# VectorE's order at the last tile of a MoE layer: the third group of experts chosen ahead of the last norms, the last router product a block later, list scatters paused at each tile

## The chip, the cores and the metric

The kernel runs on one core of one Trainium2 chip. The metric is the device time of one execution in microseconds (us), the median of the runs shown.

## What is computed

One layer of a hybrid backbone on T = 1152 tokens (1024 sample tokens and 128 prompt tokens) of width D = 1024: adaLN, a mixer (gated linear attention, a gated MLP, a short convolution, a Fourier branch), a residual with layer norm, then a mixture of 64 experts with a shared expert and a second residual with layer norm. The change lies where the mixer's output meets the mixture:

```python
x = layer_norm(DEEPNORM_ALPHA * x + g1 * y, p["ln1_g"], p["ln1_b"])
h = layer_norm(x) * (1 + sc2) + sh2
...
scores = jax.nn.sigmoid((x @ p["w_router"]).astype(jnp.float32))
biased = scores + p["router_bias"].astype(jnp.float32)
grp_score = lax.top_k(biased.reshape(t, N_GROUPS, EXPERTS_PER_GROUP), 2)[0].sum(-1)
_, top_g = lax.top_k(grp_score, TOPK_GROUPS)
gmask = jnp.any(top_g[:, :, None] == jnp.arange(N_GROUPS)[None, None, :], axis=1)
masked = jnp.where(jnp.repeat(gmask, EXPERTS_PER_GROUP, axis=1), biased, -jnp.inf)
_, idx = lax.top_k(masked, TOP_K)
w = jnp.take_along_axis(scores, idx, axis=1)
...
return (jax.nn.silu(xb @ p["w_exp_gate"][e]) * (xb @ p["w_exp_up"][e])) @ p["w_exp_down"][e]
...
shared = (jax.nn.silu(x @ p["w_sh_gate"]) * (x @ p["w_sh_up"])) @ p["w_sh_down"]
return (routed + shared).reshape(bsz, n, d)
```

Each token goes to 8 of 64 experts, which come from 4 of 8 groups. The assignments are sorted by expert and cut into blocks of 128 rows, each padded to one expert.

## The kernel before, in words

**Tiles and blocks.** Tokens are cut into NT = 9 tiles of 128. Each engine has its own program, written out by hand; what stands in an engine's code runs in that order, and semaphores tie the engines together. Matrix products are made from a high and a low part of each operand, three products for one: `gate_up_high`, `x_high`, `h_high`, `down_high` are ScalarE's copies of the high part, `gate_up_low`, `x_low`, `h_low` VectorE's and `down_low` GpSimd's subtractions for the low part.

**The norms' loop (up to 618 us).** For each tile TensorE makes the output projection (L2058), VectorE takes it out of PSUM (`x1_sum`, L1079), makes the first layer norm (`x1_norm`) and the modulated second one (`h2_norm`); ScalarE computes each norm's square sum and square root in between (`ln_std`, L666 and L668). TensorE turns `h2` (`transpose_h2`, L810), ScalarE copies it (`copy_h2T`, L675), TensorE makes the router product (`route`, L821), ScalarE takes the logits out (`logits_out`, L650) and applies the sigmoid to a group of tiles (`route_scores`, L655).

**The groups.** Tiles are routed in five groups, `RG = [(0, 2), (2, 4), (4, 6), (6, 8), (8, 9)]`. For a group g VectorE chooses the experts (`choose(g)`, which is `choose_groups`, L990 to L1001, and `choose_experts`, L1014 to L1033), TensorE counts each token's rank within its expert (`rank(g)`, L799 and L801), VectorE turns ranks into places (`place(g)`, L1042 to L1051, semaphore `dest_ready`), and GpSimd scatters token number and weight into a list in DRAM (`fill_lists(g)`, L576, 8 scatters of 128 rows for each tile). All 72 scatters land in a list that is then read back by two gathers (L593).

**The shared blocks (b = 0 to 8).** The nine tiles go through the shared expert: `turn_x` (L898, eight transposes), `gate_up` (L843, 24 products), `turn_h` (L875), `down` (L843, 12 products, two blocks behind). The remaining norms, choices and ranks are put between the steps of these blocks. At b = 8 TensorE turns the list (`lists`, L852), VectorE copies the token numbers (L1161) and releases the first gathers of expert rows (`next_gather`, L1144; GpSimd L601). A block's `x_low` must be done before TensorE may turn the next one (`xT_ready`).

**The routed blocks.** The same steps follow for some 104 gathered blocks in expert order, with the weights of each expert streamed in by SP (L456, L457, L460). SP loads into a half of the raw buffer once `gate_up_low` of what was in it is done (`gu_low`). From here on the loop's code is untouched.

## Time and profile before

| | us |
|---|---|
| median of 3 runs | 1849.58 |
| lowest and highest run | 1846.86, 1855.94 |
| the profiled execution | 1866.22 |
| its span | 1864.5 |
| TensorE busy in it | 1707.2 (92%) |
| VectorE, ScalarE, GpSimd busy | 925.0, 844.7, 771.6 |
| mean granted TensorE clock, of full speed | 0.961 |

All rows below are of the profiled execution. PE is TensorE, DVE VectorE, ACT ScalarE, POOL GpSimd, SP SyncE. A timeline's row gives the start, the duration, the engine, the line of the code, the operation with its operands, how many instructions it stands for, and in brackets how long the engine had been idle before it and what released it.

### The profile page before, as it was taken

What the parts mean: (1) busy time and instruction counts of PE and PEld (TensorE: products, weight loads), DVE (VectorE), ACT (ScalarE), POOL (GpSimd) and SP (SyncE); (2) the same over time, 40 slices, a digit from 0 to 9 for tenths busy, and PEclk for the clock granted to TensorE, in tenths of its full rate; (3) what the DMA queues carried; (4) which work ended last, traced back from release to release, by engine and by line L of the source; (5) the groups of instructions that cost most, each with busy time, mean ns of one, the idle gap of its engine ahead of it and who ended that gap; (6) DMA issues with size and microseconds to landing.
All of it is one profiled execution on the core that took longest, in us unless ns stands there. A gap on an engine that the chain in (4) does not pass through costs nothing.

```text
span 1864.5 us, 30719 instructions
## 1 busy us (share of the span) xinstructions
PE 1707.2 (92%) x8566; PEld 1335.3 (72%) x8567; DVE 925.0 (50%) x1432; ACT 844.7 (45%) x956; POOL 771.6 (41%) x452
## 2 busy tenths in 40 slices
PE   5899999999899777999999989999999989999845
PEld 1667678888455665888877878888878768888631
DVE  6522310157578853564464455334644654465529
ACT  0521012251033422675575667445765765567622
POOL 4520000400003553475456656535665556546530
PEclk9899999999999888999999999999999989999878
DMA  9505531022542443599799899966998899889786
GB/s 350 182 12 177 168 121 37 26 91 71 201 178 97 154 135 123 215 321 295 225 294 305 262 301 335 290 174 195 327 323 247 274 303 322 260 258 301 247 257 268
DMA packets 104719, 406.50 MB, mean 218 GB/s; under 512 B 17836, under 2 KB 36393, under 8 KB 76512
## 3 DMA queue, kind: packets, MB, share of 16 engines
q1 hardware_dynamic: 64656, 288.82, 41.8%
q0 software_dynamic: 37424, 107.59, 23.7%
q10 hardware_dynamic: 2592, 9.44, 1.7%
q8 instruction: 32, 0.52, 0.1%
q14 instruction: 15, 0.12, 0.0%
HBM read 339.94 MB, written 84.72 MB: 228 GB/s over the span
## 4 chain that ended last, share of the span: by engine, by line
PE 61%; DMA 16%; DVE 7%; issue 6%; ACT 5%; POOL 2%; SPq 1%; ACTq 1%; POOLq 0%; DVEq 0%
PE ps L843 32%; PE ps L1917 11%; DMA arena<-hx_dram,arena 6%; PE ps L898 4%; PE ps L2058 4%; DMA raw<-w_exp_up 3%; DMA acc_dram<-arena 3%; PE ps L1865 2%; DMA wvs_raw<-w_in 2%; POOL d_split L582 1%; ACT gu_split L640 1%; ACT d_split L645 1%; PE ps L2048 1%; PE ps L1890 1%; PE ps L875 1%
## 5 line engine op out<-in xcount | busy, mean ns | idle before, releaser
L843 PE MATMUL ps<-gu_split,xT 128*128 (+1 forms) x2712 | 641.4, 392 | 5.8 <-issue 5.7
L843 PEld LDWEIGHTS ps<-gu_split,xT 128*128 128x128 f32 x2712 | 511.9, 189 | 116.7 <-issue 10.0
L843 PE MATMUL ps<-d_split,hTe 128*128 (+1 forms) x1356 | 358.0, 415 | 33.1 <-ACT arena L721 33.1
L582 POOL TENSOR_TENSOR d_split<-raw,d_split (+1 forms) x65 | 299.5, 4608 | 201.1 <-ACT d_split L645 200.4
L974 DVE TENSOR_TENSOR gu_split<-raw,gu_split (+1 forms) x130 | 294.3, 2305 | 127.7 <-ACT gu_split L640 123.7
L843 PEld LDWEIGHTS ps<-d_split,hTe 128*128 128x128 f32 x1356 | 259.5, 198 | 88.6 <-issue 36.7
L640 ACT ACTIVATE gu_split<-raw (+1 forms) x130 | 241.4, 1908 | 63.1 <-SPq L484 36.5
L601 POOL DMA_INDIRECT arena<-hx_dram,arena x108 | 137.9, 1277 | 191.2 <-DVE arena L1144 159.0
L1138 DVE TENSOR_TENSOR arena<-ps,arena 128x256 f32<-128x256 f32 x113 | 70.5, 624 | 284.0 <-ACT arena L727 282.9
L610 POOL DMA_INDIRECT acc_dram<-arena x104 | 170.0, 1635 | 86.3 <-DVE arena L1149 56.1
L1917 PE MATMUL ps<-hT_split,w_split 128*128 128x512 f32 (+1 forms) x816 | 192.3, 394 | 3.7 <-DVE w_split L1599 3.7
L1128 DVE TENSOR_TENSOR xT<-ps,xT 128x1024 fp32r<-128x1024 f32 x115 | 140.8, 1224 | 103.9 <-ACT xT L699 103.9
L1917 PEld LDWEIGHTS ps<-hT_split,w_split 128*128 128x128 f32 x816 | 151.9, 190 | 41.5 <-issue 6.9
L721 ACT ACTIVATE arena<-ps,arena 128x1024 f32<-128x1024 f32 x104 | 115.4, 1109 | 120.9 <-DMA acc_dram<-arena 64.7
L699 ACT ACTIVATE xT<-ps 128x1024 fp32r<-128x1024 f32 x115 | 118.1, 1027 | 69.6 <-PE ps L898 61.6
L898 PE MATMUL ps<-const,arena 128*128 128x128 f32 x920 | 123.4, 278 | 26.0 <-DMA arena<-hx_dram,arena 18.0
L576 POOL DMA_INDIRECT list_dram<-arena x72 | 79.3, 1101 | 155.5 <-DVE arena L1051 135.0
L727 ACT ACTIVATE arena<-ps 128x256 f32<-128x256 f32 x113 | 43.0, 381 | 205.0 <-PE ps L843 198.3
L2058 PE MATMUL ps<-arena 128*128 128x512 f32 x288 | 126.9, 594 | 2.9 <-DVE arena L1079 2.3
L645 ACT ACTIVATE d_split<-raw (+1 forms) x65 | 124.0, 1908 | 7.2 <-SPq L488 4.9
L898 PEld LDWEIGHTS ps<-const,arena 128*128 128x128 f32 x920 | 106.2, 143 | 29.0 <-issue 12.7
L2058 PEld LDWEIGHTS ps<-arena 128*128 128x128 f32 x288 | 53.5, 190 | 65.1 <-issue 61.2
(287 smaller groups left out, 1437.7 us busy)
## 6 DMA issues: line engine op xcount, KB each, us to landing
raw<-w_exp_gate SPq DMA_DIRECT2D x64, 1024.0 KB
raw<-w_exp_up SPq DMA_DIRECT2D x64, 1024.0 KB
raw<-w_exp_down SPq DMA_DIRECT2D x64, 1024.0 KB
arena<-w_ada SPq DMA_DIRECT2D x16, 1024.0 KB, 4.9
arena<-x_dram SPq DMA_DIRECT2D x18, 512.0 KB, 11.4
arena<-acc_dram SPq DMA_DIRECT2D x18, 512.0 KB, 11.5
arena<-w_ada SPq DMA_DIRECT2D x4, 2048.0 KB, 27.5
w_raw<-w_in SPq DMA_DIRECT2D x16, 512.0 KB, 4.9
```

What stands on the lines that cost most here:

```text
L582: tt(d_split(q, 1), raw_d(q), d_split(q, 0).bitcast(F32), ALU.subtract).then_inc(d_low, 1)
L601: pool.indirect_dma_start(out=xg[:, p, :], out_offset=None, in_=hx_dram, in_offset=bass.IndirectOffsetOnAxis(ap=gidx[:, p:p + 1], axis=0), ...
L610: pool.indirect_dma_start(out=acc_dram[p], out_offset=bass.IndirectOffsetOnAxis(ap=sidx[:, p:p + 1], axis=0), in_=yb[:, p, :], in_offset=N ...
L640: a(gu_split(q, 0, half * (GU // 2), GU // 2), raw_gu(q, half), ACT.Copy).then_inc(gu_high, 1)
L645: a(d_split(q, 0), raw_d(q), ACT.Copy).then_inc(d_high, 1)
L699: a(xT[:, p, 0, :].rearrange("p (h x) -> p h x", h=2), ps[:, 0:2, :], ACT.Copy).then_inc(xT_high, 1)
L843: last = mm(dst, lhs(a, j), rhs(b, j), start=(t == 0), stop=(t == len(terms) - 1))
L898: last = pe.transpose(ps[:, c // 4, (c % 4) * P:(c % 4 + 1) * P], xg[:, p, c * P:(c + 1) * P], ident)
L974: last = tt(part(1), raw_gu(q, half), part(0).bitcast(F32), ALU.subtract)
L1128: tt(two(xT[:, p, 1, :]), ps[:, 0:2, :], two(xT[:, p, 0, :].bitcast(F32)), ALU.subtract).then_inc(xT_ready, 1)
L1917: last = mm(dst, lhsT, rhs, start=(t == 0), stop=(t == len(terms) - 1))
L2058: last = mm(ps[:, 2 * (i % 2) + h, :], yT[:, j, tile(i)], w_out[:, j, h * 512:(h + 1) * 512], start=(start and j == chunks[0]), stop=(j == 1))
```

## The change

On VectorE `choose(2)` leaves the norms' loop. It stood ahead of `x1_sum(8)`; now `x1_sum(8)`, `gate_up_low(0)` and `x_low(0)` come first, then `choose(2)`, `x_low(1)`, `place(2)` and `x1_norm(8)`, and `h2_norm(8)` comes after block 0's step. The choice of the last group is made in one piece in block 3, and `gate_up_low(1)` goes from block 7 to block 8, behind the copy of the lists. TensorE turns the last `h2` in block 1 and makes its router product in block 2, ScalarE's copies, logits and scores follow. On GpSimd `fill_lists` can take part of a group, waits before each tile but the first until all earlier scatters have landed (`list_out`), and `down_low(0)` stands between tiles 4 and 5.

```diff
-            def fill_lists(g):
+            def fill_lists(g, i0=0, i1=NT):
 
                 pool.wait_ge(dest_ready, g + 1)
-                for i in range(*RG[g]):
+                for i in range(max(i0, RG[g][0]), min(i1, RG[g][1])):
+                    if i:
+                        pool.wait_ge(list_out, 16 * TOPK * i)
                     for k in range(TOPK):
...
             fill_lists(0)
             fill_lists(1)
+            fill_lists(2, 4, 5)
             down_low(0)
-            for g in range(2, 5):
-                fill_lists(g)
+            fill_lists(2, 5, 6)
+            fill_lists(3)
+            fill_lists(4)
...
                 if b == 0:
-                    ln_std(2 * NT - 2, x1[:, (NT - 1) % 2, :])
                     logits_out(NT - 2)
                 else:
-                    ln_std(2 * NT - 1, x1[:, (NT - 1) % 2, :])
                     route_scores(3)
-                    act.wait_ge(h2_ready, NT)
-                    down_high(0)
+                    ln_std(2 * NT - 2, x1[:, (NT - 1) % 2, :])
 
             def shared_step(b, p):
                 silu(b, p)
-                if b == 0:
+                if b == 1:
                     copy_h2T(NT - 1)
-                if b == 1:
                     act.wait_ge(x1_out[0], 16 * 5)
                     act.wait_ge(x1_out[1], 16 * 4)
-                if b == 1:
+                if b == 2:
                     logits_out(NT - 1)
                 if b >= 1:
                     h_high(b - 1, 1 - p)
-                if b == 1:
+                if b == 2:
                     route_scores(4)
                 if b + 2 < NT:
                     x_high(b + 2, p)
+                if b == 0:
+                    ln_std(2 * NT - 1, x1[:, (NT - 1) % 2, :])
+                    act.wait_ge(h2_ready, NT)
+                    down_high(0)
...
                 gate_up(b, p, -1)
-                if b == 3:
-                    rank(3)
                 if b == 0:
-                    transpose_h2(NT - 1)
                     rank(2)
                 if b == 1:
+                    transpose_h2(NT - 1)
+                if b == 2:
+                    pe.wait_ge(hT_ready, 1)
                     route(NT - 1)
                     turn_x(b + 2, p, b + 2 - NT)
                     pe.wait_ge(logit_out, NT)
                 if b >= 1:
                     turn_h(b - 1, 1 - p)
-                if b != 1 and b < NT - 2:
+                if b == 2:
+                    rank(3)
+                if b != 2 and b < NT - 2:
                     turn_x(b + 2, p, b + 2 - NT)
...
-                if i in (3, 5, 7):
+                if i in (3, 5):
                     choose(i // 2 - 1)
...
-            for b in range(2):
-                x_low(b, b)
-                if b == 0:
-                    x1_norm(NT - 1)
-                else:
-                    h2_norm(NT - 1)
+            x_low(0, 0)
+            choose(2)
+            x_low(1, 1)
+            place(2)
+            x1_norm(NT - 1)
...
-                if b == NT - 2:
+                if b == NT - 1:
                     gate_up_low(1)
-                if b == NT - 1:
                     for j in range(2):
...
                 if b == 0:
-                    place(2)
+                    h2_norm(NT - 1)
                     choose_groups(3)
                 if b == 1:
                     choose_experts(3)
                 if b == 2:
-                    choose_groups(4)
                     place(3)
                 if b == 3:
-                    choose_experts(4)
+                    choose(4)
```

VectorE at the last tile, before, from the end of choice 2 (L1033) to the end of `h2_norm(8)` (L1107). L1079 is `x1_sum(8)`, L974 `gate_up_low(0)`, L1128 an `x_low`, L1087 to L1092 `x1_norm(8)`:

```order
L1033 TENSOR_TENSOR arena<-arena 128x128 [waits dve_step]
L1079 TENSOR_TENSOR arena<-ps,arena 128x1024 [waits x1_out0,w3_mm,dve_step]
L974 TENSOR_TENSOR gu_split<-raw,gu_split 128x2048 [waits gu_high] x2
L1128 TENSOR_TENSOR xT<-ps,xT 128x1024 [waits xT_high]
L1087 SCALAR_TENSOR_TENSOR arena,small<-arena 128x1024 [waits x0r_in0,y3_used]
L1062 TENSOR_SCALAR small<-small 128x1 [waits xa_raw]
L1090 SCALAR_TENSOR_TENSOR arena<-arena,small 128x1024 [waits mean_ready]
L1069 RECIPROCAL small<-small 128x1 [waits std_ready,dve_step]
L1092 SCALAR_TENSOR_TENSOR arena,small<-arena,small 128x1024 [waits dve_step]
L1128 TENSOR_TENSOR xT<-ps,xT 128x1024 [waits xT_high]
L1062 TENSOR_SCALAR small<-small 128x1 [waits x1_ready]
L1101 SCALAR_TENSOR_TENSOR arena<-arena,small 128x1024 [waits mean_ready]
```

The same place now, from the end of choice 2 (L1039) on. L1134 is an `x_low`, L1048 to L1057 `place(2)`, L1093 the start of `x1_norm(8)`:

```order
L1039 TENSOR_TENSOR arena<-arena 128x128 [waits dve_step]
L1134 TENSOR_TENSOR xT<-ps,xT 128x1024 [waits xT_high,dve_step]
L1048 TENSOR_TENSOR arena<-ps,const 128x128 [waits rank_mm]
L1049 TENSOR_TENSOR arena<-arena 128x128 [waits dve_step]
L1051 MAX arena<-arena 128x8 [waits dve_step]
L1051 MAX arena<-arena 128x8
L1053 TENSOR_SCALAR arena<-arena 128x16 [waits dve_step]
L1055 TENSOR_TENSOR arena<-arena 128x1024
L1056 TENSOR_TENSOR arena<-arena 128x1024 [waits dve_step]
L1057 TENSOR_REDUCE arena<-arena 128x16 [waits dve_step]
L1093 SCALAR_TENSOR_TENSOR arena,small<-arena 128x1024 [waits x0r_in0,y3_used]
```

`x1_sum(8)`, `gate_up_low(0)` and `x_low(0)` moved ahead of the choice, and `x_low(1)` and `place(2)` stand between the choice and the norms.

VectorE at block 8, before: gate and `h_low` of the block ahead (L1138, L1133), `gate_up_low(1)` (L974), the lists' copies (L1161 to L1164), then block 8 with two `x_low` (L1128):

```order
L1133 TENSOR_TENSOR hTe<-ps,hTe 128x256 [waits hT_high]
L974 TENSOR_TENSOR gu_split<-raw,gu_split 128x2048 [waits gu_high] x2
L1161 CAST arena<-ps 128x144 [waits list_t]
L1144 COPY arena<-arena 128x1 [waits dve_step]
L1144 COPY arena<-arena 128x1
L1164 COPY arena<-ps 128x144
L1138 TENSOR_TENSOR arena<-ps,arena 128x128x2 [waits dve_step,sg_ready]
L1133 TENSOR_TENSOR hTe<-ps,hTe 128x256 [waits hT_high]
L1128 TENSOR_TENSOR xT<-ps,xT 128x1024 [waits xT_high]
```

And now (L980 is `gate_up_low(1)`, L1166 to L1169 the lists' copies, L1134 `x_low(9)`):

```order
L1139 TENSOR_TENSOR hTe<-ps,hTe 128x256 [waits hT_high]
L1166 CAST arena<-ps 128x144 [waits list_t]
L1150 COPY arena<-arena 128x1 [waits dve_step]
L1150 COPY arena<-arena 128x1
L1169 COPY arena<-ps 128x144
L1144 TENSOR_TENSOR arena<-ps,arena 128x128x2 [waits dve_step,sg_ready]
L1139 TENSOR_TENSOR hTe<-ps,hTe 128x256 [waits hT_high]
L980 TENSOR_TENSOR gu_split<-raw,gu_split 128x2048 [waits gu_high] x2
L1134 TENSOR_TENSOR xT<-ps,xT 128x1024 [waits xT_high]
```

`gate_up_low(1)` moved from ahead of the lists' copies to between block 8's `h_low` and `x_low(9)`.

## Rows read from the trace of the kernel before

**Rows 1.** Timeline of TensorE around the last tile.

```profile
618.70 1.09 PE L810 MATMUL ps<-const,arena 128*128 128x128 f32 x8
627.46 1.97 PE L898 MATMUL ps<-const,arena 128*128 128x128 f32 x8 [7.67 <-DVE arena L1079]
...
642.64 1.10 PE L810 MATMUL ps<-const,arena 128*128 128x128 f32 x8 [1.30 <-DVE arena L1107]
```

**Rows 2.** Timeline of VectorE: choice 2 and what follows, then `place(2)`.

```profile
618.49 0.27 DVE L990 TENSOR_TENSOR arena<-arena 128x128 f32<-128x128 f32 x1
...
626.18 1.22 DVE L1079 TENSOR_TENSOR arena<-ps,arena 128x1024 f32<-128x1024 f32 x1
...
649.24 0.28 DVE L1042 TENSOR_TENSOR arena<-ps,const 128x128 f32<-128x128 f32 x1
...
654.00 0.28 DVE L990 TENSOR_TENSOR arena<-arena 128x128 f32<-128x128 f32 x1
```

**Rows 3.** Timeline of ScalarE: a table load ahead of a square root.

```profile
577.89 1.28 ACT L668 ACT_TABLE_LOAD   x1
```

**Rows 4.** Timeline of TensorE, then of ScalarE and VectorE, 667 to 719 us.

```profile
667.98 0.26 PE L801 MATMUL ps<-arena 128*128 128x64 bf16 x3
...
677.40 0.67 PE L875 MATMUL ps<-const,arena 128*128 128x128 f32 x2
677.86 1.92 PE L898 MATMUL ps<-const,arena 128*128 128x128 f32 x8
...
693.14 1.29 PE L843 MATMUL ps<-gu_split,xT 128*128 128x512 f32 x5
...
708.48 0.38 PE L875 MATMUL ps<-const,arena 128*128 128x128 f32 x2
...
712.74 5.76 PE L843 MATMUL ps<-gu_split,xT 128*128 128x512 f32 x24
...
674.28 1.02 ACT L711 ACTIVATE arena<-ps 128x1024 f32<-128x1024 f32 x1 [12.45 <-issue]
...
705.89 0.15 DVE L1202 TENSOR_SCALAR arena<-ps 64x1 int32<-64x1 f32 x1 [11.90 <-remote]
```

**Rows 5.** Timeline of GpSimd: list scatters, the first and last of a batch, another's last.

```profile
654.36 0.97 POOL L576 DMA_INDIRECT list_dram<-arena  x1 [5.13 <-DVE arena L1051]
...
673.45 0.96 POOL L576 DMA_INDIRECT list_dram<-arena  x1 [0.30 <-issue]
...
702.10 0.95 POOL L576 DMA_INDIRECT list_dram<-arena  x1 [0.30 <-issue]
```

**Rows 6.** DMA queue q0 (packets, MB, engine share): 655 to 660, 674 to 676, 755 to 756.

```profile
q0 software_dynamic: 38, 0.00, 0.6%
...
q0 software_dynamic: 32, 0.00, 1.3%
...
q0 software_dynamic: 1, 0.00, 0.1%
```

**Rows 7.** Timeline at the lists: TensorE, VectorE, GpSimd, and SP's weight load.

```profile
731.54 0.73 PE L852 MATMUL ps<-const,arena 128*128 128x128 f32 x4
...
745.97 1.97 PE L898 MATMUL ps<-const,arena 128*128 128x128 f32 x8 [7.82 <-DMA arena<-hx_dram,arena]
...
752.02 5.73 PE L843 MATMUL ps<-gu_split,xT 128*128 x24
...
731.24 4.49 DVE L974 TENSOR_TENSOR gu_split<-raw,gu_split 128x2048 fp32r<-128x2048 f32 x2 [1.12 <-ACT gu_split L640]
735.65 0.30 DVE L1161 CAST arena<-ps 128x144 int32<-128x144 f32 x1
...
737.06 1.04 POOL L601 DMA_INDIRECT arena<-hx_dram,arena  x1 [10.12 <-DVE arena L1144]
...
751.24 0.99 POOL L601 DMA_INDIRECT arena<-hx_dram,arena  x1 [11.84 <-DVE arena L1144]
...
735.93 0.35 SPq L456 DMA_DIRECT2D raw<-w_exp_gate  x1
```

## The prediction, made before the changed kernel was run

> **What bounds the kernel now.** First the page: TensorE is busy for 1707 of 1864.5 us. A gain must therefore come out of TensorE's idle time or its slow clock. The change touches one stretch only, from the last tile's projection (618 us) to the first routed experts (752 us), so I read that stretch on each engine.
>
> On TensorE [rows 1] the reader is to see three kinds of hole. One: after the transposes at 618.70 it waits until 627.46 for `x1_sum(8)`, which stands on VectorE behind the choice of group 2; it waits once more, 1.3 us, until 642.64 for `h2_norm(8)`. Two: at 668 and 694 us it creeps. Three: at the first gathered block it waits from 738.1 to 745.97 for a gather.
>
> VectorE's own row of work [rows 2] runs without a gap to speak of from 618.49 to 642.6: the choice of group 2 takes 7.7 us (618.49 to 626.18), then come `x1_sum` 1.2, `gate_up_low(0)` 4.5, the norms and two `x_low` of 1.2. So in the first part VectorE sets the pace and TensorE waits for it.
>
> The creep [rows 4] is stranger. From 667.98 to 677.40 TensorE gets out the rest of `rank(3)`, 15 small products at 0.05 us each; from 693.14 to 708.48 it needs 15.3 us for 24 products that take 5.7 elsewhere (712.74). Nothing is waited for (the timeline calls it issue); the matmuls of one accumulation, with no semaphore between them, go out one to three at a time every 0.7 or 1.4 us. ScalarE stands 12.45 us in the first and VectorE 11.90 us in the second, while GpSimd keeps issuing list scatters 0.30 us apart [rows 5], one every 1.26 us, and the DMA engines are nearly idle (1.3% from 674 to 676 [rows 6]). Both creeps begin 10 to 14 us after a batch of 16 scatters has begun (the first at 654.36) and end 2 to 3 us after its last one (674.4 and 703.1). Two batches before 640 us show no creep. Price of the two: 9.4 − 0.8 = 8.6 and 15.3 − 5.7 = 9.6 us, and the halved clock after the first adds 0.9 for eight transposes (1.92 for 1.04 us) and as much for the down product behind them: 20.0 us in this execution.
>
> **How this execution stands to the median.** The profiled run took 1866.2 us (span 1864.5), the three timed ones 1846.9, 1849.6 and 1855.9. It is 16.6 us over their median, and without the creeps it would be 1846.2 us, at the lower end of their reach. A creep that lets a trickle of unrelated instructions through on three engines looks like the taking of records being slow, not like work being slow. I take it that the timed runs have no creeps. No row shows that directly; it is the choice on which the forecast rests.
>
> The Trainium skill bears on this choice (NOTIFIC — the notification-queue block, section 7.1): inside the block that writes trace records the pipeline holds back the producer sooner than lose a record. That would make the creeps a cost of profiling, and would put the change at the forecast below; if they were the kernel's own, the first rival's time would hold. No run here shows the block itself.
>
> **Part 1, VectorE's order at the last tile (loses 5).** `x1_sum(8)`, `gate_up_low(0)` and `x_low(0)` now go first, so TensorE's turn of block 0 starts at about 622 instead of 627.5. But choice 2 (7.7 us) and `place(2)` (649.24 to 654.00: 4.8 us) now stand ahead of both norms. The last `h2_norm` ends at 642.6 now. To that come `place(2)` 4.8, `gate(0)` 0.6 and `x_low(2)` 1.2, since `h2_norm` moved behind block 0's step, and ScalarE's tables: sigmoid for group 3, square root, silu for block 0 and square root again alternate on the norms' path, three loads of 1.28 us [rows 3], with the silu itself 0.4, some 0.6 of it covered. 4.8 + 0.6 + 1.2 + 3.8 + 0.4 − 0.6 = 10.2: `h2_norm(8)` ends at 652.8.
>
> What can TensorE do until then? `turn_x(0)`, router product 7, `turn_x(1)`, `gate_up(0)`, `rank(2)`, `turn_x(2)` and `gate_up(1)`, done at about 641. Then it stands some 12 us for the transposes, which have moved down one block. Of the list of work that it had at 642.64, rank (0.4), a turn (0.9) and a gate_up (5.5) are done: 6.8 us. The clock has dropped by then ([rows 1]: eight transposes take 1.09 us at 618.70 and 1.97 at 627.46, behind an idle of 7.7), worth 1.7 us over about 4 us of work. Net at the start of block 4: +10.2 − 6.8 + 1.7 = **+5.1 us**, rounded to 5. Bounds: 3, if the tables are hidden better; 8, if TensorE meets more waits for `x_low(1)` (VectorE finishes it at 634.4, TensorE could use it at 632.7) or for weights.
>
> **Part 2, router product, scores and choices a block down (0).** Router product 8 (1.9 us) stays the same instructions; the waits of block 2 for `hT_ready` and `logit_out` are met (`h_low(0)` by 658.5, the product after 662). The choice of group 4 now goes in one piece in block 3, 5.8 us, ends by 684 and is wanted by `rank(4)` at 684.4: met within about 0.5 us. `down_high(0)` on ScalarE still waits for `h2_norm(8)`; it ends at 655, `down_low(0)` on GpSimd at 659.6, wanted at 666. Behind it stand tile 5's scatters, with 5 us of room before group 3 is placed at 674.9. SP's 5 MB of expert weights wait for the transposes and start at 656 instead of 645; they are not wanted before 720.
>
> **Part 3, the pauses (0 in the forecast).** Each pause costs the landing of the last scatter less the 0.3 us of a normal gap. Bounds [rows 5, 6]: 1.7 us (the scatter of 673.45 ends at 674.4 and has its 32 packets done by 676), and about 5 us when weights fill the engines: from 655 to 660, with a scatter out every 1.26 us, only 38 packets got through, the worth of one scatter out of five. I take 1.7, since no 3 MB load runs then. The chain: group 3 placed 674.9, tile 6 until 685.1, pause, tile 7 until 696.9, pause, tile 8 until 708.7, landed 710.3; the list's rows are known at about 710, list gathers and landing 5 us more: 715.2. TensorE comes to `lists()` at 717 to 718. Slack 2.6 us.
>
> **Part 4, `gate_up_low(1)` behind the lists (gains 3.4, less 1 for the clock).** At 731.54 TensorE turns the lists; VectorE is in `gate_up_low(1)` (731.24, 4.5 us) and copies them only at 735.65, the first gather goes out at 737.06, 5.5 us after the lists, and then shares the DMA engines with 3 MB of weights that SP issued at 735.93, when that same `gate_up_low(1)` was done [rows 7]. It lands 8.9 us later. Now counted from the lists' start t: copy at t+0.8, gather out at t+2.2, landed about t+6.0 to 6.5 (a gather out at 751.24 without weights has its packets done by 755 [rows 6], 3.8 us), TensorE ready for it at t+6.6: no wait. `turn_x(9)` and a down until t+10.4. But `x_low(9)` now stands behind `gate_up_low(1)`: gate 8 done t+7.9, +4.5, +1.2 = t+13.6, so `gate_up(9)` starts at t+14.6. Now it starts at 752.02 = t+20.5. Gain 5.9. The weights then start at t+12.6 and the third gather at t+15; by the first gather's rate (all landed 10 us after SP's issue) it lands at t+23.3, wanted at t+20.9: 2.4 back. Two idles near 3 us may each halve the clock for a while: 1.0 back. **−5.9 + 2.4 + 1.0 = −2.5 us**, bounds −6 and 0.
>
> **Sum.** +5 − 2.5 = **+2.5 us**. In the profile's frame, if the creeps leave its execution: 1866.2 − 20.0 + 2.5 = 1848.7. For the median: 1849.6 + 2.5 = **1852 us**. What comes later is a shift of the same routed loop: the loads of expert 3 arrive some 11 us before they are wanted.
>
> **Rivals.** *The creeps are real and the pauses end them* (0.25). For it: they fall into scatter batches and end with them. Against: early batches had none, and the timed runs are short by about their price. Then 1849.6 − 20.0 + 2.5: 1832 us. That the pauses do nothing to real creeps gives the forecast's time again and is counted with it.
>
> *The lists come late* (0.12). If the two pauses before tiles 7 and 8 cost the upper bound, 2 × 3.4 = 6.8 us are added against 2.6 of slack, and the list gathers add as much as 2 if they meet the blocks' output writes; it decides from 1.3 us per pause over my 1.7. TensorE then stands 4 to 6 us at block 8 and runs at the low clock behind it, 2 more: 1852 + 6 to 8, with the front's upper bound of 3 more **1860 us**, slower.
>
> **How the numbers follow.** Forecast 0.63, rivals 0.25 and 0.12. The range 1831 to 1861 takes in the forecast with its bounds (+3 to +8, −6 to 0, and the timed runs' own spread of −3 and +6), half of each rival. A measurement of this kernel tells 0.5%, 9 us, from no change. Faster by more: most of the first rival and a little of the forecast, 0.25. Slower by more: half of the second, and a tenth of the forecast where front and timed spread add up, 0.14. Within: 0.61.
>
> **What would show it.** In the changed kernel's rows: the transposes of the last `h2` start near 653, TensorE having stood about 12 us before them (wrong if under 5 us: then part 1 is mis-sized); the first wait near 627 gone; no issue gaps of 1.4 us inside the blocks; GpSimd's scatters in eights with gaps near 2 us (above 4: second rival); `gate_up(9)` some 15 us after the lists instead of 20.5. The forecast is wrong if timed runs fall by 15 us or more: then the creeps were in them.

## The result and the profile after

The changed kernel takes 1861.54 us (median of 9 runs, 1859.38 to 1869.64), the kernel before beside it 1849.22 (9 runs, 1841.03 to 1855.94): 1.0079 times as long, 95% interval 1.0063 to 1.0096. It is 12.3 us slower. The forecast was 1852 with a range up to 1861, so the time lies above the forecast and just outside the range.

The profiled run of the changed kernel took 1860.9 us (span 1859.1), within 1 us of its timed median. It reaches this stretch 4.54 us later than the profile of before: the transposes of tile 7 start at 623.24, against 618.70 in [rows 1]. I subtract that wherever I compare, and call such times aligned.

TensorE, timeline of the changed kernel (columns: start us, us, engine, line, operation, out<-in, shapes, count, [idle before <-what ended it]):

```profile
623.24 1.09 PE L814 MATMUL ps<-const,arena 128*128 128x128 f32 x8
...
657.65 1.97 PE L814 MATMUL ps<-const,arena 128*128 128x128 f32 x8 [11.88 <-DVE arena L1113]
...
728.12 1.02 PE L856 MATMUL ps<-const,arena 128*128 128x128 f32 x4 [6.59 <-DMA arena<-list_dram,arena]
729.07 7.92 PE L847 MATMUL ps<-gu_split,xT 128*128 128x512 f32 x24
...
743.99 1.94 PE L902 MATMUL ps<-const,arena 128*128 128x128 f32 x8 [3.15 <-DVE xT L1134]
745.59 6.59 PE L847 MATMUL ps<-gu_split,xT 128*128 x24
...
754.72 1.09 PE L902 MATMUL ps<-const,arena 128*128 128x128 f32 x8 [2.33 <-DMA arena<-hx_dram,arena]
...
758.40 5.61 PE L847 MATMUL ps<-gu_split,xT 128*128 x24
```

The reader is to see, in order: the stand of 11.88 us for the last tile's `h2`, as forecast; no `issue` gaps, where [rows 4] had 20 us of slow going; then, new, 6.59 us of waiting for the lists, and `gate_up(8)` behind it, part of it at the lower clock (7.92 us for 24 products with a mean granted clock of 0.70; 5.76 us in [rows 4]). `gate_up(9)` comes 17.5 us after the lists' turn, not 20.5, but `gate_up(10)` comes 30.3 us after it.

GpSimd, timeline of the changed kernel, the scatters that follow a pause and the first list gather:

```profile
682.53 0.97 POOL L578 DMA_INDIRECT list_dram<-arena  x1 [8.37 <-DMA list_dram<-arena]
...
698.36 0.96 POOL L578 DMA_INDIRECT list_dram<-arena  x1 [6.03 <-DMA list_dram<-arena]
...
712.58 0.95 POOL L578 DMA_INDIRECT list_dram<-arena  x1 [4.42 <-DMA list_dram<-arena]
...
724.53 0.99 POOL L597 DMA_INDIRECT arena<-list_dram,arena  x1 [2.17 <-DMA list_dram<-arena]
```

GpSimd stands 8.37, 6.03 and 4.42 us for landings ahead of tiles 6, 7 and 8. The forecast said near 2, and "above 4: second rival". So the first reading was that the second rival had come true, and that the slow issue (the prediction's creeps: instructions that wait for nothing and still go out in steps) belonged to profiled runs alone. The experiments confirmed the one and refuted the other.

### The profile page after: what moved, and what is told of

The parts are those of the page before. It is cut to its first block, busy times and chain, and to the rows that moved or that the text cites. A ratio compares the mean times of both kernels' runs of the same rounds, so it can differ in the third digit from the quotient of the medians.

```text
span 1859.1 us, 30726 instructions
## 1 busy us (share of the span) xinstructions
PE 1706.4 (92%) x8566; PEld 1335.2 (72%) x8567; DVE 929.3 (50%) x1432; ACT 848.3 (46%) x959; POOL 769.4 (41%) x452
## 4 chain that ended last, share of the span: by engine, by line
PE 63%; DMA 18%; DVE 5%; POOL 4%; issue 4%; ACT 3%; SPq 1%; ACTq 1%; POOLq 0%; DVEq 0%
PE ps L847 31%; PE ps L1920 11%; PE ps L2061 6%; DMA arena<-hx_dram,arena 5%; DMA raw<-w_exp_up 5%; PE ps L902 4%; DMA acc_dram<-arena 3%; DMA arena<-w_ada 2%; POOL list_dram L578 2%; PE ps L1868 2%; POOL d_split L584 1%; DMA list_dram<-arena 1%; PE ps L2051 1%; PE ps L1893 1%; ACT d_split L649 1%
## 5 line engine op out<-in xcount | busy, mean ns | idle before, releaser
L980 DVE TENSOR_TENSOR gu_split<-raw,gu_split (+1 forms) x130 | 294.3, 2305 | 127.2 <-ACT gu_split L644 127.2
L1134 DVE TENSOR_TENSOR xT<-ps,xT 128x1024 fp32r<-128x1024 f32 x115 | 140.8, 1224 | 96.3 <-ACT xT L703 96.3
L902 PEld LDWEIGHTS ps<-const,arena 128*128 128x128 f32 x920 | 105.6, 143 | 18.5 <-issue 15.8
```

The costliest lines, as they stand in the source:

```text
L902: last = pe.transpose(ps[:, c // 4, (c % 4) * P:(c % 4 + 1) * P], xg[:, p, c * P:(c + 1) * P], ident)
L980: last = tt(part(1), raw_gu(q, half), part(0).bitcast(F32), ALU.subtract)
L1134: tt(two(xT[:, p, 1, :]), ps[:, 0:2, :], two(xT[:, p, 0, :].bitcast(F32)), ALU.subtract).then_inc(xT_ready, 1)
```

## Experiments

Every run was timed beside the kernel before on its own chip, and these chips fall into two kinds. On some the kernel before takes 1848 to 1849 us, on others 1870 to 1873; I call the second **slow-issue chips**, for what their traces show. The runs e0, f and g were made on chip 14 and the runs h on chip 11, both without slow issue; e1 to e4 on chip 8 and the runs k on chip 2, both with it. Only chip 14 was used at two times (f and g), so for the slow ones the runs can't tell the chip from the time at which it was used.

### The kernel before, and the changed one, on other chips

Neither has an edit; e0 is the kernel before.

> The kernel before, unchanged, for its profile. If the slow issue is in every run of it that takes about 1870, the profiled time agrees with the timed median beside it within 5 us and the trace has issue gaps of 0.7 to 1.4 us in some 20 us of TensorE's time. If it is in profiled runs alone, the profiled time lies some 17 to 20 us above the timed median. If it is neither, TensorE's stretch from 655 to 712 has no issue gaps.

> The changed kernel as it is, timed once more beside the kernel before. If the slow issue of TensorE (20 us in the stretch around 668 and 694 us) is in the timed runs of a chip on which the kernel before takes 1870, the changed kernel, which has none of it, stays at about 1861 there, 0.995 times the kernel before; then the sign of the change hangs on whether the slow issue occurs. If the kernel before is at 1849 again in these runs, 1.008. Rival: the two chips differ by 1% in everything, and the changed kernel takes 1882 where the kernel before takes 1870.

> The changed kernel as it is. On a chip where the kernel before takes 1870 (with slow issue): 1861 to 1866, 0.995 to 0.998, so faster there by what the pauses cost less than the 20 us that they save. On a chip where it takes 1849: 1862 to 1866, 1.008 to 1.010, as twice before.

> The changed kernel. Where the kernel before takes 1870: 1861 to 1866, 0.995 to 0.998. Where it takes 1849: 1861 to 1866, 1.007 to 1.010.

| run | kernel before beside it | changed kernel | ratio (95%) |
|---|---|---|---|
| f1 | 1848.60 | 1866.32 | 1.0099 (1.0070 to 1.0128) |
| h1 | 1848.41 | 1861.42 | 1.0074 (1.0048 to 1.0100) |
| k1, slow-issue chip | 1872.89 | 1867.07 | 0.9972 (0.9949 to 0.9995) |

e0 was a profile taken beside f1: 1851.24 us. Busy times of each engine from 660 to 712 us (columns: us, then busy us and count on PE, PEld, DVE, ACT, POOL, then the granted clock, DMA share, GB/s), first in the profile that stands ahead of the prediction:

```profile
660.00:712.00 52.00, 38.54 (x182) 29.84 (x181) 24.10 (x74) 9.26 (x13) 28.16 (x30) 0.80 0.29 72
```

and the same program in e0:

```profile
660.00:712.00 52.00, 51.02 (x278) 41.61 (x276) 31.07 (x90) 16.76 (x23) 35.55 (x37) 1.00 0.44 102
```

Of one program, TensorE runs 278 operations in that stretch in the one execution and 182 in the other. TensorE in e0 has no issue gap at all there, though its GpSimd issues 40 scatters in the same rhythm without a stop (653.88 to 703.32). So the slow issue is no cost of recording alone: e0 was recorded too and lacks it. On the slow-issue chips it is in the timed runs, since there the profiled runs that show it agree with timed medians: e3 below, the kernel before with one step moved, has 14 gaps (12.3 us) in a profiled run of 1871.87 us, and its timed median is 1872.25. The timed runs given with the kernel before, 1849.58, were without it and the profile beside them was with it; that they are from different chips fits all this, but isn't recorded. Late loading of instructions isn't borne out as the cause either: in the profile of before the two DMA queues that carry instructions (q8, q14) moved nothing between 664 and 691 us, the whole of the first creep, and from 640 to 730 us they have 6 packets there and 7 in e0.

k1 gives the sign: where there is slow issue, the same change makes the kernel 0.28% faster, not 0.79% slower. k1's trace has five issue gaps on TensorE, 2.0 us together (the profile of before: 13.3 us in twelve). That is not all that is left. VectorE stood 4.73 us ahead of `place(2)`, though TensorE's counts for it were done as early as in the result's trace, where it stood 0.92 us. VectorE in k1, then in the result:

```profile
636.58 0.29 DVE L1048 TENSOR_TENSOR arena<-ps,const 128x128 f32<-128x128 f32 x1 [4.73 <-remote]
```

```profile
639.43 0.29 DVE L1048 TENSOR_TENSOR arena<-ps,const 128x128 f32<-128x128 f32 x1 [0.92 <-PE ps L805]
```

The last `h2` is on the path behind it, so TensorE stands 15.81 us for it instead of 11.9, and is ready for the lists 7.4 us later than in the result's trace (105.7 and 98.3 us in the table below). In the changed kernel the pauses so cut the slow issue from 15 us (without them e1 is ready for the lists at 112.6 us, g2 at 97.6) to some 7; with the pauses alone (e2, below) none is left. The change isn't faster by 20 us there, as the first rival had it, for these 7 us, because VectorE's order costs its 5 here too, and because TensorE then waits 6.88 us for the lists.

### The pauses alone, and the change without them

Edit of e2 and g1, to the kernel before (e1 and g2 take the same two lines out of the changed kernel):

```diff
                 for i in range(*RG[g]):
+                    if i:
+                        pool.wait_ge(list_out, 16 * TOPK * i)
                     for k in range(TOPK):
```

> The changed kernel with the waits between the list scatters taken out again; all else stays as changed. My theory (the pauses made the lists late: TensorE stood 6.6 us for the lists at 728 us and ran the 7.92 us block at half clock instead of 5.74): these 8.8 us come back, so about 1853, 1.002 times the kernel before (VectorE's new order costs 5, the moved gate_up_low(1) gives back 2 to 3). First rival (TensorE's 20 us of slow issue near 668 and 694 us belong to timed runs too, and the pauses end them): they return, about 1870. Second rival (the pauses cost nothing and VectorE's order costs it all): 1861, as with the pauses. By my theory and by the first rival alike the profiled run may show the slow issues again; only by mine it then lies some 17 us above the timed runs.

> The kernel before with nothing but the waits between the list scatters. My theory: a pause takes 4.4 to 6.0 us, of which up to four lie in the stretch that leads to the lists (before tiles 5 to 8), each taking the place of 1.3 us between scatters; tiles 5 and 6 start with group 3 near 655 us aligned and end near 684, so the lists come some 10 to 18 us after TensorE is ready: 1859 to 1868. First rival (slow issue is in the timed runs and the pauses end it): 1829 plus those 10 to 18, 1839 to 1847. Second rival (pauses cost nothing): 1849.

> The kernel before with nothing but the waits between the list scatters, once more, in the hope of a chip on which the kernel before takes 1849 and shows no slow issue. There my theory says: the lists come 20 us after TensorE is ready (20.47 in its first profile, which had no slow issue either), of which some 6 to 7 are given back since gate_up_low(1) and the weights are then out of the way (gate_up(10) 22.4 us after the lists instead of 28.9): about 1849 + 19.5 - 6.5, 1862, the same absolute time as on the chip with the slow issue. Rival (pauses cost nothing by themselves): 1849. If the kernel before takes 1870 again, 1863 as the first time.

> The changed kernel without the waits between scatters, once more. Where there is no slow issue, my theory says: TensorE at the lists 5 to 7 us later than before and waiting 1 to 2 us for them, gate_up(10) some 29 us behind the lists as before: 1854 to 1856 where the kernel before takes 1849, 1.003. The changed kernel itself took 1861.5 and 1866.3 beside a kernel before of 1849, so the pauses make 7 to 12 of its 12 to 18 us and VectorE's order 5 to 7. Rival (VectorE's order costs all of it): 1862 to 1866. Where the kernel before takes 1870: 1871 as the first time.

Measured: on a slow-issue chip (kernel before 1870.56) pauses alone 1863.12, ratio 0.9953 (0.9932 to 0.9975), and the change without pauses 1871.51, 0.9988 (0.9968 to 1.0008). On a chip without (1848.77) pauses alone 1863.28, 1.0078 (1.0058 to 1.0098), and the change without pauses 1858.06, 1.0046 (1.0031 to 1.0062). With the pauses alone the kernel takes the same 1863 on either kind of chip. e2's trace has no issue gap on TensorE, and TensorE is ready for the lists 92.3 us after the transposes of tile 7, as in e0 (92.4): the pauses end the slow issue where there is one, and cost 14.5 us where there is none. TensorE and GpSimd in g1:

```profile
738.15 1.02 PE L854 MATMUL ps<-const,arena 128*128 128x128 f32 x4 [22.42 <-DMA arena<-list_dram,arena]
739.10 8.07 PE L845 MATMUL ps<-gu_split,xT 128*128 128x512 f32 x24
...
751.84 5.75 PE L845 MATMUL ps<-gu_split,xT 128*128 x24
...
761.29 5.61 PE L845 MATMUL ps<-gu_split,xT 128*128 x24
```

```profile
674.43 0.96 POOL L578 DMA_INDIRECT list_dram<-arena  x1 [5.50 <-DMA list_dram<-arena]
...
690.81 0.97 POOL L578 DMA_INDIRECT list_dram<-arena  x1 [6.55 <-DMA list_dram<-arena]
...
705.27 0.96 POOL L578 DMA_INDIRECT list_dram<-arena  x1 [4.66 <-DMA list_dram<-arena]
...
719.58 1.05 POOL L578 DMA_INDIRECT list_dram<-arena  x1 [4.51 <-DMA list_dram<-arena]
```

Four pauses of 4.5 to 6.6 us, each in place of 0.3, are 20.0 us, and TensorE stands 22.42 us for the lists, where e0 stands 0.98. Of these 21.4 us 5.7 come back: `gate_up(10)` follows the lists by 23.1 us, in e0 by 28.8. That give-back was not in my sum.

### VectorE's order alone

h4 is the changed kernel without the pauses and with `gate_up_low(1)` in its old place, so the order at the last tile is all that is left:

```diff
-                    if i:
-                        pool.wait_ge(list_out, 16 * TOPK * i)
...
+                if b == NT - 2:
+                    gate_up_low(1)
                 if b == NT - 1:
-                    gate_up_low(1)
                     for j in range(2):
```

> The changed kernel without the waits and with gate_up_low(1) in its old place: VectorE's order of the last tile's norms and the third group's choice, with what goes with it on TensorE and ScalarE, is all that differs from the kernel before. On a chip without slow issue: TensorE 5.3 us later at the lists, and gate_up(10) 28.8 us behind them as before: 1854, 1.003. If the place of gate_up_low(1) is what the version without waits lost beside that, this one is at 1854 and that one at 1858; if not, this one is at 1858 too. On a chip with slow issue: 1869 to 1872.

Measured 1854.62 against 1848.41, 1.0032 (1.0010 to 1.0054), that is 6 us. The timeline of h4's TensorE shows the stand, and its arrival at the lists without any wait:

```profile
651.69 1.97 PE L812 MATMUL ps<-const,arena 128*128 128x128 f32 x8 [11.89 <-DVE arena L1111]
...
715.25 0.73 PE L854 MATMUL ps<-const,arena 128*128 128x128 f32 x4
...
729.61 1.97 PE L900 MATMUL ps<-const,arena 128*128 128x128 f32 x8 [7.75 <-DMA arena<-hx_dram,arena]
```

Counted from the transposes of tile 7, it is ready for the lists at 97.9 us, e0 at 92.4: 5.5 us, for which the forecast had 5. g2 (1.0046) has an interval that overlaps h4's (1.0032), and its trace is no longer by the last column of the table below, so these runs can't tell its 9 us from h4's 6.

### `gate_up_low(1)`: behind the lists, in the gap, or ahead

e3 is the kernel before with it moved as the change does; e4 and g4 put it right behind the copies of the lists, where VectorE stands idle; g3 is the changed kernel with it back in its old place.

```diff
                     dve.nop().then_inc(lists_ready, 1)
+                    gate_up_low(1)
                 gate(b, p)
...
-                if b == NT - 2:
-                    gate_up_low(1)
```

> The kernel before with gate_up_low(1) moved behind the lists alone, as the change does. My theory: gate_up(9) follows the lists at 17.5 us instead of 20.5 and its clock is less halved: 2.5 to 3 us faster, about 1846.5. Rival: the transfers for the block after are what ends last there, no difference, 1849.

> The kernel before with gate_up_low(1) put right behind VectorE's copies of the lists, where VectorE stands while the gathers run. If VectorE's conversion is what gate_up(9) waits for, gate_up(9) starts some 6 to 9 us sooner after the lists than before: about 1841 to 1843. Rival: the gathers of x for block 9 or the weights end last there, and no more than the 2.5 us of the later place come back: 1846.5.

> The kernel before with gate_up_low(1) right behind the copies of the lists, once more. Its first profile had gate_up(10) 26.4 us behind the lists instead of 28.9: 2.5 to 4 us faster than the kernel before, 0.998, on any chip. Rival: no difference.

> The changed kernel with gate_up_low(1) put back to its old place, two blocks ahead of the lists' use. I had taken 2.5 us of gain for its move. Now my theory says the move is a loss as soon as the lists are late, since VectorE stands idle while TensorE waits for them: in the kernel with pauses alone gate_up(10) followed the lists by 22.4 us, in the changed kernel by 30.3 and 29.7. Putting it back gives 7 us: about 1855 to 1858 on any chip. Rival (the move gains 2.5 as predicted): 2.5 slower than the changed kernel, 1864 to 1869.

e3: 1872.25 against 1870.56, 0.9997 (0.9974 to 1.0020), no gain. e4: 1866.54, 0.9973 (0.9952 to 0.9993), and g4: 1846.57 against 1848.77, 0.9986 (0.9970 to 1.0002). g3: 1860.61, 1.0068 (1.0048 to 1.0089); f1, the changed kernel on the same chip at another time, was 1.0099 (1.0070 to 1.0128). That is some 5 us less, with intervals that overlap, and only 1 us less than the 1861.5 of the result and of h1: that putting it back saves time is likely, how much is open. TensorE in e0, then in g4, then in g3, from the lists to `gate_up(10)`:

```profile
711.58 0.81 PE L852 MATMUL ps<-const,arena 128*128 128x128 f32 x4 [0.98 <-DMA arena<-list_dram,arena]
...
724.94 1.97 PE L898 MATMUL ps<-const,arena 128*128 128x128 f32 x8 [6.66 <-DMA arena<-hx_dram,arena]
...
731.05 5.72 PE L843 MATMUL ps<-gu_split,xT 128*128 x24
...
740.43 5.61 PE L843 MATMUL ps<-gu_split,xT 128*128 x24
```

```profile
712.45 0.81 PE L852 MATMUL ps<-const,arena 128*128 128x128 f32 x4 [0.90 <-DMA arena<-list_dram,arena]
...
721.00 1.09 PE L898 MATMUL ps<-const,arena 128*128 128x128 f32 x8 [1.86 <-DMA arena<-hx_dram,arena]
...
727.49 1.09 PE L898 MATMUL ps<-const,arena 128*128 128x128 f32 x8 [2.65 <-DMA arena<-hx_dram,arena]
...
737.95 5.61 PE L843 MATMUL ps<-gu_split,xT 128*128 x24
```

```profile
730.92 1.02 PE L856 MATMUL ps<-const,arena 128*128 128x128 f32 x4 [13.95 <-DMA arena<-list_dram,arena]
...
744.13 5.76 PE L847 MATMUL ps<-gu_split,xT 128*128 x24
...
753.58 5.61 PE L847 MATMUL ps<-gu_split,xT 128*128 x24
```

In g3 nothing is waited for after the lists: while TensorE stood for them VectorE had done `gate_up_low(1)`. In the changed kernel it is work for after the lists, and `gate_up(10)` follows by 30.3 us instead of 22.7. The saving of 7.6, from which I had expected 7 us for the whole kernel, is not all kept. With the weight buffer free sooner SP issues the next weights at 721.21, ahead of the list gathers, and these take 7.0 us from issue (723.91) to TensorE, where f1 and e0 have 3.6 (724.32 to 727.90; 708.00 to 711.58).

Without pauses the place behind the lists gains nothing either, and g2 shows why. Its TensorE (the lists at 715.68):

```profile
730.13 5.73 PE L845 MATMUL ps<-gu_split,xT 128*128 x24
...
739.79 1.97 PE L900 MATMUL ps<-const,arena 128*128 128x128 f32 x8 [3.71 <-DMA arena<-hx_dram,arena]
741.41 4.65 PE L845 MATMUL ps<-d_split,hTe 128*128 128x512 f32 x12
745.89 5.63 PE L845 MATMUL ps<-gu_split,xT 128*128 x24
```

`gate_up(9)` comes 14.5 us after the lists, 5.0 sooner than in e0. Then TensorE stands 3.71 us for the third gather, which shares the DMA engines with the weights that SP issued at 727.98, and the transposes and the 12 products behind it run partly at the lower clock (granted clock 0.58; 1.97 and 4.65 us instead of 1.04 and 3.0). The step from `gate_up(9)` to `gate_up(10)` takes 15.8 us instead of 9.4: the 5.0 are more than used up.

g4's place wins 3.4 us by its trace and 2.2 by its medians; its interval just holds 1. With e4 it is the only version whose median lies below that of the kernel before on both kinds of chip. On a slow-issue chip it is no better than the changed kernel (e4 0.9973, k1 0.9972).

### What ends the slow issue: fewer scatters under way, or a slower pace

f2, h2 and k2 (one kernel) let a batch of four scatters go when the last but one has landed: never more than eight are under way, as with the pauses, but GpSimd hardly stops.

```diff
+                        batch, at = divmod(i * TOPK + k, 4)
+                        if batch > 1 and at == 0:
+                            pool.wait_ge(list_outs[batch % 2], 16 * 4 * (batch // 2))
...
-                                                in_=pairs[:, i, k, :], in_offset=None).then_inc(list_out, 16)
+                                                in_=pairs[:, i, k, :], in_offset=None).then_inc(list_outs[batch % 2], 16)
```

> The kernel before with two counters for the list scatters, in batches of four: a batch is issued when the last but one has landed, so at most eight scatters are under way and GpSimd hardly stops (a landing takes 4.4 to 6.0 us, the batch between takes 5.05). If the slow issue comes from how many scatters are under way, it is gone with next to no delay of the lists: about 1850 where the kernel before takes 1870. If it comes from how fast they are issued over a longer stretch, it stays: within 4 us of the kernel before.

> The kernel before with scatters in batches of four, two batches under way at most. On a chip with slow issue: if that comes from scatters under way beyond eight, it is gone and the time is about 1852, 0.990; if from pace, it stays, and the time is 1870 to 1874. On a chip without: 1850.7 as the first time, 1.001.

> The kernel before with scatters in batches of four, two batches under way at most. Where the kernel before takes 1870: 1852 if the slow issue comes from scatters under way beyond eight, 1870 to 1874 if from the pace. Where it takes 1849: 1849 to 1851.

On chips without slow issue it costs next to nothing: 1850.68 (1.0013, 0.9996 to 1.0031) and 1851.25 (1.0002, 0.9977 to 1.0026). On the slow-issue chip: 1871.78 against 1872.89, 0.9991 (0.9970 to 1.0012), with 15 issue gaps on TensorE, 12.9 us together. Busy times of k2 from 660 to 712, and a piece of its TensorE's timeline:

```profile
660.00:712.00 52.00, 38.99 (x182) 30.27 (x181) 23.84 (x77) 9.00 (x15) 28.16 (x30) 0.77 0.31 82
```

```profile
699.80 0.59 PE L848 MATMUL ps<-gu_split,xT 128*128 128x512 f32 x1 [0.90 <-issue]
701.21 1.44 PE L848 MATMUL ps<-gu_split,xT 128*128 128x512 f32 x3 [0.82 <-issue]
704.03 1.44 PE L848 MATMUL ps<-gu_split,xT 128*128 128x512 f32 x3 [1.39 <-issue]
```

GpSimd's scatters in k2 start at 655.50 and go on every 1.26 us, with 0.61 us instead of 0.3 at the only stop. So eight under way at most doesn't end the slow issue; the pauses, with the same eight, do. What they have besides is a lull after every eight, 2.7 to 4.4 us in e2. That fits a cause that builds up with the pace over a series and drains in a lull; what builds up, no run shows. How many scatters it takes isn't settled: in the profile of before the first gap comes at the eleventh, but in k1 VectorE is held ahead of `place(2)` from about the seventh after a pause of 6.65 us. The 16 scatters from 607.72 to 632.94 in the profile of before, in uneven steps of 1.3 to 3.3 us, have no gap beside them.

f3 was to change the pace alone, with eight empty instructions on GpSimd behind each scatter:

> The kernel before with eight empty instructions on GpSimd behind each list scatter, which stretch the pace from 1.26 us to an estimated 1.5 to 2 us and wait for nothing. If the slow issue comes from the pace over a longer stretch, it shrinks or goes; the lists then come 6 to 18 us later than TensorE is ready, which gives back most of it: 1855 to 1868 where the kernel before takes 1870, without issue gaps. If it comes from scatters under way beyond eight, at 1.5 us or more fewer are under way too, and the same follows, so only the run with batches tells these apart. If neither matters, issue gaps stay and the time goes up: 1872 or more.

It says nothing on the pace: 1848.92 (1.0003, 0.9987 to 1.0019), on a chip without slow issue, and the scatters went out at 651.49, 652.76 and 654.03, as fast as ever.

```profile
651.49 0.97 POOL L576 DMA_INDIRECT list_dram<-arena  x1 [5.12 <-DVE arena L1053]
652.76 0.96 POOL L576 DMA_INDIRECT list_dram<-arena  x1 [0.30 <-issue]
```

h3 joins the batches with g4's place:

> The kernel before with both: batches of four, and gate_up_low(1) right behind the copies of the lists. The lists are 9 to 10 us late by the batches, and gate_up_low(1) then has an idle VectorE ahead of the lists which this place does not use, so gate_up(10) follows the lists by 25 to 26 us, not by 22: on a chip without slow issue 1852 to 1854, worse than either alone. If the two gains add, 1848.

1845.89, 0.9986 (0.9963 to 1.0010): not the loss that I had expected, and no gain beyond g4's. TensorE waited 5.34 us for its lists, not 10. That wait is not steady: with the batches alone it was 10.23 us in f2 and 1.44 in h2, one kernel on two chips.

### The stretch in one table

Times in us from the transposes of tile 7 in each run's own trace (the first row of the fence of the changed kernel, 623.24, and its like):

| run | transposes of tile 8 | ready for lists | wait for lists | `gate_up(10)` after lists | `gate_up(10)` |
|---|---|---|---|---|---|
| e0, before | 23.9 | 92.4 | 1.0 | 28.8 | 122.2 |
| h4, order alone | 34.3 | 97.9 | 0 | 30.5 | 128.4 |
| g2, change without pauses | 34.1 | 97.6 | 0 | 30.2 | 127.9 |
| g1, pauses alone | 23.9 | 92.3 | 22.4 | 23.1 | 137.9 |
| g3, change, `gate_up_low(1)` in old place | 34.6 | 98.2 | 14.0 | 22.7 | 134.8 |
| changed kernel (result) | 34.4 | 98.3 | 6.6 | 30.3 | 135.2 |
| h1, changed kernel | 34.4 | 98.0 | 6.7 | 30.0 | 134.7 |
| f1, changed kernel | 34.6 | 98.2 | 10.6 | 29.7 | 138.4 |
| g4, low in the gap | 23.9 | 92.4 | 0.9 | 25.5 | 118.8 |
| profile of before (slow issue) | 23.9 | 112.8 | 0 | 29.9 | 142.8 |
| k1, changed kernel (slow issue) | 38.2 | 105.7 | 6.9 | 29.5 | 142.1 |
| k2, batches (slow issue) | 23.9 | 114.1 | 0 | 30.8 | 144.9 |

The last column of the changed kernel less that of e0 is 13.0 us; the medians differ by 12.3. In f1 it is 16.2, the medians 17.7.

## Why the prediction was wrong

**The creeps.** The choice on which the forecast rested, none in the timed runs, held for the runs of the result: with them the kernel before would be at 1870. That is luck, since the reason given for it didn't hold. The creeps go with the chip (or with the time at which it was used), not with the recording; the rule of the Trainium skill that I had called in for it (NOTIFIC — the notification-queue block, section 7.1, the trace block holding back its producers) isn't borne out as the cause by these runs, since e0 is recorded alike and has none, and k1 and k2 lose the time in timed runs as well. For a slow-issue chip the first rival was right in kind: the pauses end the creeps when they stand alone, and cut them to some 7 us in the changed kernel. A small slip in the reading of them: `rank(3)` has 15 small products in all, and four of these are out before the first gap.

**Part 1, VectorE's order, +5.** Right. The transposes of the last `h2` come at 657.65, 653.1 aligned, forecast near 653; the stand is 11.88, forecast some 12; TensorE comes to the lists 5.9 us later than e0, and h4 times it at 6. VectorE's wait near 627 is gone; at the same turn, which comes at 622.1 aligned, TensorE now stands 2.29 us for a load from `hx_dram`; the start itself is the forecast one, about 622.

**Part 2, 0.** Right: TensorE is 5.9 us later than e0 at `gate_up(4)` and at `gate_up(7)`, and still 5.9 when it is ready for the lists.

**Part 3, the pauses, 0. This is the step that failed.** Its term, 1.7 us for a pause, was read from when the recorded packets of a scatter were done [rows 6]. What GpSimd waits for is the landing's signal, and no row of before had that behind a list scatter. The changed kernel's trace has both: the last scatter ahead of tile 8 goes out at 707.20, its recorded packets are done by 709.0, and GpSimd is released at 712.58. On the chips without slow issue the signal came 4.1 to 4.7 us after the end of the last scatter ahead of tile 8, where the DMA engines were busy for at most a third, and 6.0 to 9.9 us after it ahead of tiles 6 and 7 of the changed kernel. At tile 6 SP's five weight loads kept the engines busy (share 1.0 in the result's trace); at tile 7 the share was 0.5 at first and 0.15 then, and no run shows what the extra 1.5 to 3 us are. (g1 has 5.5, 6.6, 4.7 and 4.5 us, e2 on a slow-issue chip 4.4, 2.7, 4.3 and 4.2.) The second error is in the same step: it counted two pauses, before tiles 7 and 8, and took tile 6 to start with group 3's placing at 674.9. SP's weights had moved from 645 to 657.8 aligned, just ahead of tile 5's scatters, and the signal of these scatters came 3.3 us after the placing. By the chain in aligned times: tile 6 at 678.0 instead of 674.9, tile 7 at 693.8 instead of 686.8, tile 8 at 708.0 instead of 698.6, first list gather at 720.0 instead of 710.3, lists at TensorE 723.6 instead of 715.2. TensorE was ready at 717.0, at the lower end of the forecast, which leaves a slack of 1.8 us instead of 2.6. The lists came 8.4 us later than forecast: 6.6 us of standing.

**Part 4, `gate_up_low(1)`, −2.5.** Wrong, and by itself, not only for the late lists. The first term was right where the lists are in time: in g2 `gate_up(9)` comes at +14.5, forecast 14.6. What was too small is what is given back, 3.4 us: TensorE stood 3.71 us for the third gather, forecast 2.4, and the low clock behind it cost 2.6 more, forecast 1.0, so that g2 has `gate_up(10)` at +30.2, e0 at +28.8. In the changed kernel `gate_up(9)` came at +17.5 (the kernel before has 20.5, e0 19.5), since `gate_up(8)` ahead of it took 7.92 us and everything behind it moved down; then came 2.33 us at the next gather, and at `gate_up(10)` the gain was gone as well (30.3). And the comparison was with a place that late lists would have made free: g1 and g3 have 23.1 and 22.7. The two edits spoil each other: pauses make VectorE idle ahead of the lists, and the move takes away the work that would fill that idle time.

**Sum.** Forecast +5 + 0 − 2.5. Measured in the trace 5.9 + 5.6 (6.6 of waiting for 1.0) + 1.5 (30.3 for 28.8) = 13.0. Of the 10.5 us between the two, part 1 makes 0.9, part 3 5.6 and part 4 4.0.

**Rival 2** was the case that came, with the right place and the right sign. That its 1860 us also fits is in part luck: it has 6 to 8 us for the late lists, where 5.6 came, up to 3 more from the front, where 0.9 came, and still the gain of part 4, which didn't come. Its chance of 0.12 was too low: the deciding point lay 1.3 us per pause above a value that no row had measured, between bounds of 1.7 and 5, and I had taken the lower bound as the value. The middle of the bounds, 3.35, is already past that point, and with the upper one the rival's 1860 follows.

## What to carry to other kernels

Before a wait for a DMA's landing is put into a chain, price it from a row in which an engine waits for a landing of that kind, under the traffic that will be there after the change; the time at which the packets are done is only a lower bound (here 709.0 against 712.58). Where the chain feeds the bottleneck, take the middle or the upper bound as the forecast when the slack is smaller than the doubt. And when a profile is 1% off its timed runs, take the profile of the same program again on another chip before a change is made against what it shows: here the same change is 0.8% slower on one kind of chip and 0.3% faster on the other.

## What the runs showed of the hardware that was not expected

- **Slow issue on some chips and not on others.** Instructions of TensorE, ScalarE and VectorE that wait for nothing go out in steps of 0.7 and 1.4 us while GpSimd issues indirect scatters every 1.26 us. It adds some 20 us to a kernel of 1850 us, in every trace of a kernel without the pauses on chips 8 and 2 and in none on 14 and 11. A lull of 2.7 to 4.4 us after every eight scatters ends it in e2; in the changed kernel (k1) 7 us are left.
- **A small operation of VectorE was held for the whole of a GpSimd operation.** In the changed kernel an operation over 128x16 took 4.48 us, and the same line over the same shape 0.18 at 632.23; it began 0.11 us after GpSimd's subtraction of 4.56 us, and they ended together. k1 has the same pair, 4.50 and 4.58 us. VectorE's timeline, then GpSimd's:

```profile
632.23 0.18 DVE L1007 TENSOR_TENSOR arena<-arena 128x16 f32<-128x16 f32 x1
...
659.74 4.48 DVE L1007 TENSOR_TENSOR arena<-arena 128x16 f32<-128x16 f32 x1
```

```profile
659.63 4.56 POOL L584 TENSOR_TENSOR d_split<-raw,d_split 128x2048 fp32r<-128x2048 f32 x1 [3.66 <-ACT d_split L649]
```

- **The same pauses differ from run to run.** Ahead of tiles 6 and 7 GpSimd stood 8.37 and 6.03 us in the result's profile, 8.32 and 6.07 in h1, but 9.91 and 7.62 in f1, which was the slower of them by 4 us of waiting for the lists. One trace each doesn't show whether that is the chip.
- **Eight empty instructions on GpSimd behind a scatter took no time that the trace shows.** Scatters in f3 start 1.26 us apart as before; whether the empty instructions reached the engine, no run shows.
